# Two reorderings in a one-core decoder trunk: page loads by halves of the last feature weights' places, and the order of steps behind two pieces and ahead of the first gate

## Time and profile before

| | |
|---|---|
| median of 3 runs | 924.0 us (923.78 to 924.64) |
| the profiled execution's own time | 923.94 us |
| its span | 922.3 us |
| busy PE, DVE, ACT, POOL | 98%, 70%, 49%, 21% |
| share of PE in the chain that ended last | 85% |
| granted clock of TensorE | 0.998 |
| layer 0's sampled stage | about 228 to 315 us of the span |
| layer 1's | about 680 to 767 us |

### The profile page before, as it was taken

How to read it: one execution, slowest core, us unless ns; L and a number is a source line. 1 busy time by engine, 2 the same in 40 slices (tenths; PEclk the granted TensorE clock), 3 DMA queues, 4 the chain that set the end, 5 groups by cost and what they waited for, 6 DMA issues and landing times.

```text
span 922.3 us, 21430 instructions
## 1 busy us (share of the span) xinstructions
PE 899.8 (98%) x7936; PEld 837.6 (91%) x7936; DVE 648.5 (70%) x1447; ACT 453.5 (49%) x896; POOL 192.4 (21%) x321
## 2 busy tenths in 40 slices
PE   6999999999999999999999999999999999999997
PEld 6999898888887799999999998898888978999996
DVE  6999766677566467656769996676766565775674
ACT  6444665565543444335543447664554444443352
POOL 1200000347658300000000000013575771000000
PEclk9999999999999999999999999999999999999999
DMA  9762985736979973333675576865669799335421
GB/s 325 295 224 105 417 346 206 295 146 188 310 226 287 286 301 144 138 138 133 245 255 209 196 301 261 308 272 230 203 183 298 242 266 339 140 146 198 159 93 52
DMA packets 66344, 209.88 MB, mean 228 GB/s; under 512 B 12192, under 2 KB 49776, under 8 KB 56256
## 3 DMA queue, kind: packets, MB, share of 16 engines
q1 hardware_dynamic: 57200, 187.67, 55.5%
q0 software_dynamic: 8896, 20.82, 7.1%
q10 hardware_dynamic: 144, 0.01, 0.0%
HBM read 202.48 MB, written 41.36 MB: 264 GB/s over the span
## 4 chain that ended last, share of the span: by engine, by line
PE 85%; SPq 5%; DMA 3%; issue 2%; DVE 2%; ACT 2%; DVEq 0%; ACTq 0%
PE bank L1047 64%; PE bank L1307 6%; SPq L871 5%; PE bank L1060 3%; DMA paged<-in_pool 2%; PE bank L1185 1%; PE bank L1177 1%; PE bank L1214 1%; PE bank L1341 1%; PE bank L1227 1%; PE bank L1437 1%; PE bank L1240 1%; ACT paged_r L1572 1%; DMA big<-in_w_tok 1%; ACT kvp L1540 0%
## 5 line engine op out<-in xcount | busy, mean ns | idle before, releaser
L1814 DVE TENSOR_TENSOR big_r<-big,paged_r 128x1024 fp32r<-128x1024 f32 (+1 forms) x160 | 194.6, 1221 | 73.8 <-ACT paged_r L1572 72.9
L1047 PE MATMUL bank<-xnT_high_r,paged_r 128*128 128x288 f32 x768 | 231.7, 302 | 0.0
L1047 PE MATMUL bank<-xnT_r,paged_r 128*128 128x288 f32 x704 | 207.7, 295 | 0.0
L1047 PE MATMUL bank<-xnT_high_r,big_r 128*128 128x288 f32 x704 | 207.1, 294 | 0.0
L1572 ACT ACTIVATE paged_r<-big 128x1024 fp32r<-128x1024 f32 (+1 forms) x160 | 166.7, 1049 | 5.0 <-DMA big<-in_w_feat 2.8
L1047 PE MATMUL bank<-short_r,big_r 128*128 128x288 f32 x568 | 167.5, 295 | 0.0
L1047 PEld LDWEIGHTS bank<-xnT_high_r,paged_r 128*128 128x128 f32 x768 | 144.0, 188 | 4.4 <-issue 2.0
L1047 PEld LDWEIGHTS bank<-xnT_high_r,big_r 128*128 128x128 f32 x704 | 132.5, 188 | 0.0
L1047 PE MATMUL bank<-short_r,paged_r 128*128 128x288 f32 x440 | 131.0, 298 | 1.3 <-DVE big_r L1814 1.2
L1047 PEld LDWEIGHTS bank<-xnT_r,paged_r 128*128 128x128 f32 x704 | 132.3, 188 | 0.0
L1047 PE MATMUL bank<-kvp_r,paged_r 128*128 128x288 f32 x440 | 130.4, 296 | 0.0
(11 more groups left out here) (350 smaller groups left out, 1806.0 us busy)
## 6 DMA issues: line engine op xcount, KB each, us to landing
big<-in_w_tok SPq DMA_DIRECT2D x13, 2048.0 KB, 9.4
big<-in_w_feat SPq DMA_DIRECT2D x12, 2048.0 KB, 8.5
big<-in_w_gate SPq DMA_DIRECT2D x10, 2048.0 KB, 8.4
out_kept_dil<-in_cache_dil SPq DMA_DIRECT2D x16, 1020.0 KB, 13.1
paged<-in_pool SPq DMA_DIRECT2D x218, 64.0 KB, 3.9
big<-in_w_up SPq DMA_DIRECT2D x12, 1024.0 KB, 8.7
paged<-in_pool POOLq DMA_DIRECT2D x166, 64.0 KB, 4.7
big<-in_kv_win SPq DMA_DIRECT2D x4, 2048.0 KB, 9.2
```

The costliest lines, as they stand in the source:

```text
L1047: last = mm(out, l, r, start=(c == 0 and i == 0), stop=(c == n - 1 and i == 2))
L1814: v.tensor_tensor(l_part[:, rest], full[:, rest], h_part[:, rest].bitcast(FP32), ALU.subtract)\
```

## The change

It does four things, in both layers. (1) Half 0 of the first pages waits for the first half of the features of its weights: keys for feature 17, values for feature 21. POOL's `("pages", 0)`, now behind feature 17, holds both halves of the first keys (waits for features 17 and 19, 8 pages and none); `("pages", 1)`, at the head of unit 15's block, half 0 of the first values; `("pages", 2)`, behind feature 23, the store, half 1 and all later pages. SP's pages move ahead likewise. (2) The load `("vA", 0)` is cut in two halves of 1792 columns, waiting for features 21 and 23. (3) Behind the pieces (0,1,1,1) and (1,0,1,1), `hpost` comes at once, and `htail` ahead of `psplit`; the steps that stood between `hid` and `hpost` follow behind. (4) `round` and `split` of the first gate's quarter 0 come ahead of `spv(0, cnew)`, `sturn(0, slc1)`, `vc 1` and `impsum 1`. The order of PE's own instructions is not changed.

```diff
@@ def next_feat():
-        return [("feat",) + feats.pop(0)] + ([("pages", 0)] if n == 20 else [("pages", 1), ("pages", 2)] if n == 23 else [])
+        return [("feat",) + feats.pop(0)] + ([("pages", 0)] if n == 17 else [("pages", 2)] if n == 23 else [])
@@ blocks
-              (14, 1): [("cpv", 0), ("gateC", 0)], (15, 0): [("cscore", 1)] + begin(), (15, 1): begin()}
+              (14, 1): [("cpv", 0), ("gateC", 0)], (15, 0): [("pages", 1), ("cscore", 1)] + begin(), (15, 1): begin()}
@@ def piece(*between):
-        return [("hid",) + z, *between] + [("hpost",) + z[0:3]] * ends + begin() + [("htail",) + z[0:3]] * ends
+        hpost, htail, ahead = [("hpost",) + z[0:3]] * ends, [("htail",) + z[0:3]] * ends, begin()
+        if z[0:3] in ((0, 1, 1), (1, 0, 1)):
+            return [("hid",) + z, *between] + hpost + ahead[0:1] + htail + ahead[1:]
+        return [("hid",) + z, *between] + hpost + ahead + htail
...
-           [("sgateA", 0), ("sscore", 1, "d4")] + piece(("cmpt", 0), ("sscore", 1, "mix"), ("sturn", 0, "win")) + \
-           [("sexp", 1, "A")] + piece() + \
+           [("sgateA", 0), ("sscore", 1, "d4")] + piece() + \
+           [("cmpt", 0), ("sscore", 1, "mix"), ("sturn", 0, "win"), ("sexp", 1, "A")] + piece() + \
...
-           [("impsum", 0), ("spv", 1, "mix"), ("sturn", 1, "anew")] + \
-           piece(("spv", 1, "anew"), ("soA", 1)) + piece() + [("kc", 1)] + \
+           [("impsum", 0), ("spv", 1, "mix"), ("sturn", 1, "anew")] + piece() + \
+           [("spv", 1, "anew"), ("soA", 1)] + piece() + [("kc", 1)] + \
...
-            ("imp", 1), ("spv", 0, "cnew"), ("sturn", 0, "slc1"), ("vc", 1), ("impsum", 1)] + splits(("gate", 0, 0), 0) + \
+            ("imp", 1)] + splits(("gate", 0, 0), 0) + [("spv", 0, "cnew"), ("sturn", 0, "slc1"), ("vc", 1), ("impsum", 1)] + \
@@ def load_pages(queue, key, z, numbers):
         if kind == "cmp" and hb == 0:
-            queue.wait_ge(*big_used(Now.layer, split_keys[which - 2]))
+            queue.wait_ge(*half_used(split_keys[which - 2], h))
@@ new
+    def half_used(key, h):
+        return PJ.is_full(("feat",) + FEATS[4 * key[1] + 2 * h + 1])
@@ SP's list of loads
-                    at_key = {("vA", 0): both("cmp", 0, 0), ("kA", 1): both("cmp", 1, 0), ("vA", 1): both("cmp", 0, 1),
+                    at_key = {("win", 0): [("cmp", 0, 0, 0)], ("vA", 0): [("cmp", 0, 0, 1), ("cmp", 1, 0, 0)],
+                              ("kA", 1): [("cmp", 1, 0, 1)], ("vA", 1): both("cmp", 0, 1),
...
+                    if key == ("vA", 0):
+                        assert place_used_by(layer, key) == [(layer, ("feat", 5))]
+                        for h in range(2):
+                            half = slice(RB * 448 * h, RB * 448 * (h + 1))
+                            sp.wait_ge(*half_used(("feat", 5), h))
+                            sp.dma_start(bigb(key)[:, half], a["v_a"][layer, 0][:, half]).then_inc(*BIG.fill(key))
+                        continue
@@ POOL's steps
-                    if s[1] == 1:
+                    if s[1] == 2:
                         pool.wait_ge(*u_state.at("all"))
                         n_new += store(o["conv_state_out"][layer], ustate[:, :, :])
-                    for page_key in page_keys[2 * s[1]:2 * s[1] + 2] if s[1] < 2 else page_keys[4:]:
+                    for page_key in (page_keys[0:2], page_keys[2:3], page_keys[3:])[s[1]]:
                         load_pages(pool, page_key, 0, numbers)
```

More of the change, by code:

```diff
@@ L602, in trunk_program @@
         big_keys += [("kA", hb), ("win", hb), ("vA", hb)]
-    BIG = Ring(nc, "big", layered(big_keys), 3, by=16, free=False, first=2, given=[(0, ("tok", 0))], restart=True)
+    BIG = Ring(nc, "big", layered(big_keys), 3, by=16, parts=lambda key: 1 + (key == ("vA", 0)), free=False, first=2, given=[(0, ("tok", 0))], restart=True)
     gate_keys = [("gate", fh, i) for fh in range(2) for i in range(3)] + [("down", nh) for nh in range(2)]
```

## The result

The changed kernel is slower: 929.12 us, median of 6 executions (927.95 to 933.0), against 924.47 (923.78 to 925.4) for the kernel before in the same series: 4.65 us between the medians. The ratio, which is taken over the single executions and not from the medians, is 1.0056 (+5.2 us), 95% interval 1.0037 to 1.0075, that is 3.4 to 6.9 us. The forecast was 925.7 with a range to 928.0; the side of its sum was right, its size was not.

A forecast was written before the change was run, and what follows sets the result against it. PE, busy 98% of the span, bounds the kernel, so only its waits count: +3.2 (POOL's empty wait) - 0.8 (first tail) - 0 (second tail) - 0.65 (gate) = +1.7 us, forecast 925.7 us, range 923.0 to 928.0.

The forecast's parts named there:

- the second tail: At kc 1: its 0.86 us wait goes, but PE waits that much longer for selected pages; kept 0, other end 1.7.
- the 0 for earlier pages: First page issues on SP, up to 10 us sooner: nothing on PE waits for them, so 0 gained.
- The empty wait on POOL: POOL's wait for feature 19 delays unit 12's scaling; PE waits 1.6 us per layer, 3.2 lost, between 2.0 and 5.2.
- Rival (c): POOL's late scaling meets DVE's split, then another two-input operation at the shared port: +3.7, 927.7 us; chance 0.15.
- rival (b): At unit 12's transposes POOL's empty wait costs nothing, kernel faster: 922.6 to 920.3 us; chance 0.10.
- The first tail and the gate: Waits at vc 0 and the first gate go: 0.8 us gained over both layers, plus 0.65 kept in layer 0.
- The gate of layer 1: First gate's 0.59 us wait goes, but PE already waits 0.35 for selected pages there: 0 kept, other end 0.59.
- rival (a): Selected pages land as much sooner as PE arrives, so tails pay whole: -0.6, 923.4 us; chance 0.17.
- rival (d): Early pages crowd other transfers, window and cached keys: worth about nothing, 925.7 us; part of the forecast, no chance of its own.

The follow-up runs named there:

- b4: Kernel before with only the first tail (vc 0's part of part 3) and the first gate (part 4) reordered: 921.91 us, ratio 0.9984.
- e0: Kernel before with parts 3 and 4 whole (both tails and the gate), no page or load moved: 921.50 us, ratio 0.9977.
- e1: Kernel before with the first tail and the gate reordered, same as b4, run once more: 921.84 us, ratio 0.9976.
- e2: Changed kernel without the second tail and without the wait for a half in which a queue has no page: 922.72 us, ratio 0.9984.
- a2: Kernel before with part 3 alone (both tails reordered): 923.36 us, ratio 0.9998.
- b2: Kernel before with the second tail alone (kc 1's part of part 3): 924.22 us, ratio 1.0003.
- b3: Kernel before with both tails reordered and three extra matmuls on PE ahead of its wait for the selected pages: 923.36 us, ratio 0.9997.
- e3: Kernel before with both tails, the gate and three extra matmuls on PE ahead of its wait for the selected pages: 923.10 us, ratio 0.9994.
- a1: Changed kernel, but a queue with no page in a half does not wait for that half: 922.86 us, ratio 1.0000 to the kernel before.
- c0: The changed kernel once more, unedited, beside other runs on their chip: 927.25 us, ratio 1.0035 to the kernel before.
- c2: Kernel before with only a wait for feature 19 on POOL added behind feature 17: 928.16 us, ratio 1.0058.
- a3: Changed kernel with parts 3 and 4 undone, so the earlier pages and the split load alone: 930.03 us, ratio 1.0066 to the kernel before.

## Why the prediction was wrong, by its own steps

The step that failed is the one of the second tail, "it will arrive 0.86 sooner and wait 0.86 longer", kept 0, together with the sum, which prices each wait at its length. The trace shows what stood in its place: behind the lengthened waits of 1.95 and 2.67 us the clock fell, 1.5 to 1.6 us each. A smaller failure is the 0 for earlier pages. The steps in order:

**The empty wait on POOL: right in place and mechanism, its size short.** The rows show 1.64 and 1.52 us of PE waiting, and the path lengthened by 1.86 and 1.73 where 1.6 each was taken (3.6 for 3.2 in sum, inside the ends of 1.0 and 2.6 a layer). The split did start earlier with POOL silent (202.98, against 202.43 + 0.87 = 203.30), and took 1.23 for 1.45; POOL, behind it, was stretched, as assumed: eight scalings in 8.14 us instead of 8 x 0.91 = 7.28. Rival (c), the worst order at the shared port, didn't occur; rival (b), no wait at all, falls with PE's waits for POOL in both layers.

**The first tail and the gate: right, if anything short.** b4 and its repetition give -1.4 and -2.2 for the 1.45 taken. The gate of layer 1 was taken at 0 because PE waited 0.35 for pages at L1437. That wait is in none of the traces of the changed kernel, b4, e0, e1 or e2, and d0, the kernel before again, has none either; in b4, e0, e1 and e2 the 0.6 of layer 1 is kept too. By the traces the term is 0.8 + 0.65 + 0.6 = 2.0, its other end.

**The second tail: nothing gained, as said, but not free.** a2, b2 and e0 against e1 show no gain, and rival (a) falls. But "kept 0" was not the end of it: the wait that is left is 0.86 longer in each layer, and that has a price of its own, below.

**"Issuing them up to 10 us sooner removes 0 from the path", and rival (d), "worth about nothing": this step failed by up to 0.9 us,** though in the medians that isn't clear of noise. It looked only at who waits for the moved pages. What the moved transfers and issues do to the later ones, for which PE does wait, was priced by a sentence on the window and the cached keys and not on the selected pages.

**A term was missing: what a wait does to TensorE's clock.** The sum has each wait at its own length. In the profiled executions, those with matmuls put ahead of this wait (b3, e3) left out, PE waited for pages at this place for 1.85 us or more nine times, and behind seven of these the granted clock fell to 0.5; of the 22 waits of 1.67 or less none had a fall behind it. Between the same instructions of PE, one fall costs 1.5 to 1.7 us, here and behind POOL's wait. In the changed kernel the waits were 1.95 and 2.67: 0.97 and 0.35 of before, 0.86 each from the second tail, and 0.12 and 1.46 from pages that came later. The second tail alone can bring them there (1.96 and 1.88 in a2). By the traces, this is how a1 can be no faster than before (922.86 against 923.22, with waits of 2.18 and 2.34) while e0, which has the same tails and gate, is 2.5 below its own group's kernel before (waits of 1.63 and 1.31). All 6 executions of the changed kernel in its first series and 9 of 12 in both had a low clock. That the idle time is what makes the clock fall isn't shown by the runs with matmuls in it, whose times and counts are within the noise; it rests on the traces.

The sum as it should have stood: +3.6 (wait), -1.45 to -2.0 (tail and gate), +0 to 0.9 (later pages), +1.5 to 3.3 (one or two falls) = +3.1 to +6.4. Measured were +4.65 between medians (+5.2 by the ratio) and, in the repetition, +4.0 (+3.2). In the repetition the two fastest executions, 925.34 and 925.68, had a mean clock of 0.997 and 0.996, so perhaps no fall; they lie 2.1 and 2.4 above their group's 923.27, about the 3.6 - 1.45 = 2.15 that is left without one.

The mean clocks of all executions allow a second estimate. One fall takes 1.7 us of full clock (the rows at 658 to 664 us), 0.0018 of the mean. The executions of c0 lie 0.0015 below those of the kernel before beside them, c2's 0.0016 and a3's 0.0025, that is about 0.8, 0.9 and 1.4 falls each, or 1.3, 1.4 and 2.1 us. With the other terms that gives c0 +3.5, a3 +5.7 and up to 0.9 more for later pages, and c2 +5.0, where the medians have +4.0, +6.8 and +4.9. For c2 this fits in the mean only: of its five executions the two at 0.998, 928.04 and 928.16, are as slow as the one of 928.10 at 0.995, and the profiled one shows no fall before the end (span 926.4, +4.1). That part stays open.

Of the change, then, keep the first tail and the gate: b4 and e1, 921.9 and 921.8, are faster than both kernels, and so is e0, 921.5, though its second tail makes the wait for pages longer and gains nothing that can be told.

## What to carry to other kernels

A wait that guards nothing on its own queue still holds all that is queued behind it on an engine that works in order: when a list of loads is cut finer, ask of each queue whether it has a share in the new piece, and skip the wait where it hasn't. A wait removed ahead of one for a transfer isn't free even when it gains nothing: the two merge into one long wait, so look in the trace for what the granted clock does behind waits of that length, and don't price it by the length alone. And before pricing an earlier transfer at nothing, look at the next transfers for which somebody does wait, not only at the moved one.

## What the runs showed of the hardware that was not expected

- TensorE's granted clock fell to 0.50 for over 3 us behind single waits of 1.85 to 2.67 us in a kernel in which PE is 97 to 98% busy (seven of nine), and behind two of eight waits of 1.52 to 1.67 us at another place. Each fall cost 1.5 to 1.7 us. The same kernel has it in one execution and not in the next.
- At the kernel's end, where PE waits 0.46 and 0.56 us between short groups of matmuls, the clock fell in all 18 profiled executions, sometimes before PE's last matmuls (1.79 us instead of 1.04) and sometimes behind them.
- Seventeen issues of SP, those of the selected pages behind the second window's load, took from 10.16 us (e3, layer 1) to 12.82 us (the changed kernel, layer 1), with the same code around them.
- The kernel's start, up to the same wait of PE at about 104 us, took 103.8 to 105.3 us by chance, as much as several of the effects sought; only times between the same instructions told them apart in single executions.
